# Attention by half-pairs: scores issued one half earlier on TensorE, copies of the turned probabilities one half later on ScalarE

## What is computed

```python
def one_block(args):                       # x tokens: 128 queries, local keys and context
    s_loc = jnp.where(mi, jnp.einsum('bqkgd,bskd->bkgqs', qi, ki), NEG_INF)
    s_ctx = jnp.einsum('bqkgd,bckd->bkgqc', qi, kc)
    p = jax.nn.softmax(jnp.concatenate([s_loc, s_ctx, sink_col], axis=-1), axis=-1)
    return (jnp.einsum('bkgqs,bskd->bqkgd', p[..., :n_loc], vi)
            + jnp.einsum('bkgqc,bckd->bqkgd', p[..., n_loc:n_loc + n_ctx], vc))
# context tokens: the same over the 256 context keys alone
...
mx = jnp.split((silu_c @ ada_w[i] + ada_b[i])[:, None, :], N_MOD, axis=-1)   # modulation
```

## Time and profile before

| What | us |
|---|---|
| median of 3 runs | 1977.81 (1974.31 to 1981.27) |
| the profiled execution | 1977.15 |
| its span on the profile | 1975.4 |
| PE busy | 1661.9 (84%) |
| DVE busy | 1138.1 (58%) |
| ACT busy | 855.2 (43%) |
| mean granted TensorE clock | 0.915 of full |
| the attention, first scores to first matmul of w_o | 126 to 331 |

### The profile page before, as it was taken

One profiled execution on the slowest core, in us unless ns is written; L12 is line 12 of the kernel. 1 busy time (PEld: TensorE's weight loads), 2 busy tenths in 40 slices (PEclk: granted clock), 3 DMA queues, 4 the chain that ended last, 5 costly groups with the idle time before them and its releaser, 6 DMA issues.

```text
span 1975.4 us, 23995 instructions
## 1 busy us (share of the span) xinstructions
PE 1661.9 (84%) x8586; PEld 1327.3 (67%) x8586; DVE 1138.1 (58%) x1780; ACT 855.2 (43%) x1286; POOL 16.8 (1%) x34
## 2 busy tenths in 40 slices
PE   3977777679999996888567999678787798998988
PEld 1853334568888885777456999566565686877768
DVE  2334444354444445678876666565546467777866
ACT  3223333442222333477554554424323265655653
POOL 1000000000000000000001000000000000000000
PEclk8988898879999998899787999778888699999999
DMA  8275552213323332132242666322211078878784
GB/s 304 70 295 175 193 212 85 65 33 96 106 87 104 96 96 64 43 97 85 74 128 88 189 187 184 111 71 83 78 55 41 29 239 274 283 259 272 264 287 160
DMA packets 201823, 279.57 MB, mean 142 GB/s; under 512 B 12314, under 2 KB 111116, under 8 KB 195596
## 3 DMA queue, kind: packets, MB, share of 16 engines
q1 hardware_dynamic: 200064, 269.90, 42.5%
q0 software_dynamic: 1152, 8.39, 1.1%
q10 hardware_dynamic: 524, 0.19, 0.0%
HBM read 277.40 MB, written 1.05 MB: 141 GB/s over the span
## 4 chain that ended last, share of the span: by engine, by line
PE 60%; DVE 21%; DMA 10%; ACT 6%; issue 3%; ACTq 0%; SPq 0%; DVEq 0%; POOL 0%; POOLq 0%
PE bank L390 47%; DMA stage<-in_w_dram 8%; DVE weights_lo L363 4%; PE bank L518 3%; ACT weights_hi L351 2%; PE bank L962 2%; DVE softmax_cols L1912 2%; DVE work L1932 1%; PE bank L946 1%; PE bank L1262 1%; PE bank L563 1%; DMA work<-in_c_ctx_dram 1%; DVE work L596 1%; DVE x_and_ctx L599 1%; PE bank L1312 1%
## 5 line engine op out<-in xcount | busy, mean ns | idle before, releaser
L363 DVE TENSOR_TENSOR weights_lo<-stage,weights_hi 128x1024 fp32r<-128x1024 f32 x428 | 515.8, 1222 | 158.7 <-ACT weights_hi L351 149.9
L351 ACT ACTIVATE weights_hi<-stage 128x1024 fp32r<-128x1024 f32 x428 | 442.4, 1056 | 231.6 <-DMA stage<-in_w_dram 120.6
L390 PE MATMUL bank<-act_hi,weights_hi 128*128 128x256 f32 (+1 forms) x976 | 317.4, 325 | 20.2 <-DVE x_and_ctx L2011 12.8
L390 PE MATMUL bank<-act_lo,weights_hi 128*128 128x256 f32 (+1 forms) x976 | 316.0, 324 | 0.0
L390 PE MATMUL bank<-act_hi,weights_lo 128*128 128x256 f32 (+1 forms) x976 | 315.6, 323 | 0.0
L390 PE MATMUL bank<-weights_hi,ff_hi 128*128 128x512 f32 x560 | 220.3, 393 | 11.5 <-DVE weights_lo L363 9.4
L390 PE MATMUL bank<-weights_hi,act_hi 128*128 128x512 f32 (+1 forms) x488 | 202.9, 416 | 31.7 <-DVE weights_lo L363 15.8
L390 PE MATMUL bank<-weights_hi,ff_lo 128*128 128x512 f32 x560 | 218.2, 390 | 0.0
L390 PE MATMUL bank<-weights_lo,ff_hi 128*128 128x512 f32 x560 | 218.1, 390 | 0.0
L390 PEld LDWEIGHTS bank<-act_hi,weights_hi 128*128 128x128 f32 x976 | 189.8, 194 | 36.0 <-issue 22.1
L390 PEld LDWEIGHTS bank<-act_lo,weights_hi 128*128 128x128 f32 x976 | 189.9, 195 | 13.6
(11 more groups left out here) (338 smaller groups left out, 1957.2 us busy)
## 6 DMA issues: line engine op xcount, KB each, us to landing
stage<-in_w_dram SPq DMA_DIRECT2D x192, 512.0 KB, 4.8
stage<-in_mlp_w_dram SPq DMA_DIRECT2D x128, 512.0 KB, 4.1
ada_rows_in<-in_ada_w_dram SPq DMA_DIRECT2D x40, 1024.0 KB, 5.1
stage<-in_w_in_dram SPq DMA_DIRECT2D x32, 512.0 KB, 4.0
stage<-in_lru_w_in_dram SPq DMA_DIRECT2D x20, 512.0 KB, 3.9
ada_rows_in<-in_ada_w_dram POOLq DMA_DIRECT2D x8, 1024.0 KB, 13.5
stage<-in_attn_w_qkv_dram SPq DMA_DIRECT2D x12, 512.0 KB, 5.0
stage<-in_lru_w_out_dram SPq DMA_DIRECT2D x10, 512.0 KB, 4.7
```

What stands on the lines that cost most here:

```text
L351: act.eng.activation(whi[u % NRING][:], stage[u % NSTAGE][:], ACT.Copy).then_inc(sem("hi_ready"), 1)
L363: dve.eng.tensor_tensor(wlo[u % NRING][:], stage[u % NSTAGE][:], whi[u % NRING][:].bitcast(F32), ALU.subtract).then_inc(sem("lo_ready"), 1)
L390: m = pe.eng.matmul(ps, l, r, start=start and j == 0, stop=stop and j == 2, skip_group_check=True)
```

## The change

On PE, `scores(0)` stands ahead of the loop and turn h issues `scores(h + 1)`. `values` of a pair moves from the odd turn to the even turn behind it, and the loop has one more turn. On ACT the copies of the turned half stand one turn later (half h-2 in turn h), and their wait for `values` moves with them. On DVE the split of the output moves to the even turn. The operations, their shapes, the buffers and the banks stay as they are.

```diff
--- before.py
+++ after.py
@@ -980,13 +980,14 @@
                                          skip_group_check=True)
                 m.then_inc(*pe.fill(("O", b)))
 
-            for h in range(34):
-                if h < 32:
-                    scores(h)
+            scores(0)
+            for h in range(35):
+                if h < 31:
+                    scores(h + 1)
                 if h - 1 in ADA_TURN:
                     ada_cols_pe(pe, ADA_TURN[h - 1], 7)
-                if h >= 3 and h % 2:
-                    values((h - 3) // 2)
+                if h >= 4 and h % 2 == 0:
+                    values((h - 4) // 2)
                 if 1 <= h < 33:
                     turn_probs(h - 1)
                 if h < 32:
@@ -1513,7 +1514,7 @@
                 turned_x(n)
                 if n < 2:
                     keep_ctx(n + 1)
-            for h in range(33):
+            for h in range(34):
                 if h < 32:
                     nk = P * len(key_tiles(HALVES[h][3]))
                     at = 2 * (h % 2)
@@ -1528,15 +1529,15 @@
                                      accum_out=sm[:, 1, at + i:at + i + 1]).then_inc(*act.free(("S", h, i)))
                     s.wait_ge(sem("sink_arg"), h + 1)
                     s.activation(sm[:, 2, at:at + 2], sm[:, 2, at:at + 2], ACT.Exp).then_inc(*act.mark("exps"))
-                if h:
-                    a = HALVES[h - 1][2]
-                    for n in range(len(key_tiles(HALVES[h - 1][3])) // 2):
-                        s.wait_ge(*act.filled(("PT", h - 1, n)))
-                        if h >= 3:
-                            s.wait_ge(*act.filled(("O", (h - 3) // 2)))
-                        ps = plan.bank(("PT", h - 1, n))
+                if h >= 2:
+                    a = HALVES[h - 2][2]
+                    for n in range(len(key_tiles(HALVES[h - 2][3])) // 2):
+                        s.wait_ge(*act.filled(("PT", h - 2, n)))
+                        if h >= 4:
+                            s.wait_ge(*act.filled(("O", (h - 4) // 2)))
+                        ps = plan.bank(("PT", h - 2, n))
                         s.activation(pT[:, 2 * n:2 * n + 2, a, :], ps[:].rearrange("p (k t) -> p k t", k=2),
-                                     ACT.Copy).then_inc(*act.free(("PT", h - 1, n)))
+                                     ACT.Copy).then_inc(*act.free(("PT", h - 2, n)))
                 if h in ADA_TURN:
                     ada_act(act, ADA_TURN[h])
                 if h == 28:
@@ -1931,8 +1932,8 @@
                     for i in range(2):
                         v.tensor_scalar(prob[g % 3][:, i, 0:nk], prob[g % 3][:, i, 0:nk], sm[:, 3, at + i:at + i + 1],
                                         None, ALU.mult).then_inc(*dve.mark("p_norm"))
-                if h >= 3 and h % 2:
-                    b = (h - 3) // 2
+                if h >= 4 and h % 2 == 0:
+                    b = (h - 4) // 2
                     j, c, _, qt = HALVES[2 * b]
                     v.wait_ge(*dve.filled(("O", b)))
                     ov = plan.bank(("O", b))[:, 0:256].rearrange("p (i t) -> p i t", i=2)
```

## The result

The changed kernel takes 1922.57 us (median of four runs, 1920.53 to 1923.48) against 1978.88 us of the kernel before on the same chip: the ratio is 0.9717, 95% interval 0.9697 to 0.9737. The profiled execution took 1921.84 us (span 1920.1), 55.3 us less than that of before.

The account below looks back on a forecast made before the run. Bound: the attention's ring of scores, maximum, scaling and turning, then TensorE's mixed clock. w_o at 285 instead of 331 us gains 46, less 4 for low clock: 42; 1977 - 42 = 1935 us, range 1923 to 1957.

Parts of the forecast that it names:

- everything behind 331 us moves along: Stages behind the attention, from w_o on, only start earlier; no gain or loss of their own was counted.
- the rest of the low level adds 4: Attention, 159 us from 126.3 to 285: remaining low-clock time adds 4 us, so the gain is 42.
- The ring and its cut: Attention: scores, maximum, scaling, turning wait in a loop, 6.33 us a long lap, 4.44 short; scores ahead remove it.
- The pair of turns: Attention: two long turns take 10.0 us instead of 12.66, two short ones 7.1 instead of 8.88.
- The three added waits: Attention: turning waits for copies, copies for values, odd maximum for DVE's output read; 0.7 us idle PE each turn.
- The parts of the sum: Attention at full clock: turn 4 at 142.8, turn 16 at 207, turn 30 at 270.4, w_o at 285 us.
- The clock: TensorE in the attention: granted clock near 0.97 instead of 0.88, PE's longest regular idle 0.7 us instead of 2.95.
- (1): Attention clock stays as mixed as now, 0.87: gain 22, 1955 us; chance 0.26 together with (2).
- (3): Attention slower: same ring with PE at its low level, 1984 us at clock 0.75; chance 0.04.
- (2): Attention hand-offs cost double or ACT is late: pairs 11.5 and 8.0 us, 1950 us; chance 0.26 together with (1).
- (4): Attention: bank 4 ties turn_probs(h-1) to exp(h), so laps stay: 1977 us; chance 0.04.
- (5): Attention better than written: full clock and hand-offs hidden, gain 46 + 9, 1922 us; chance 0.09.

Follow-up runs that it names:

- the filled kernel: Kernel before, in its own order, with needless matmuls into bank 4 while PE waits for the scaled probabilities: 1953.57 us, ratio 0.9887.
- the windows of 146 to 186 us shown above: From the kernel before with scores one half ahead, modulation steps ahead of turn_probs, and ACT's copy of the sums ahead of the turned half's: 1905.78 us, ratio 0.9643.

## Why the prediction was right, and where it was wrong

Two steps failed: *everything behind 331 us moves along* (8.0 us of the miss stand there), and *the rest of the low level adds 4* (these 4 us are most of the other 5.3). The mechanism of the change was right. Part by part:

*The ring and its cut*: right, and shown by three kernels. Scores ahead alone give the gain, the copies alone lose 27 us, and in the changed kernel the waits of L1912 and L962 moved as said.

*The pair of turns*: right. 9.77 us measured for 10.0 forecast, 6.85 for 7.1. The three added waits stand where the text put them, with 0.85 us of idle PE in the even turn and 0.34 in the odd one for my 0.7 in each. The pair is shorter in the odd turn, whose maximum starts with the even turning (159.09) and not 0.25 us behind it: DVE reads the output in 0.8 us (168.05 to 168.85) while PE waits 0.85.

*The parts of the sum*: turn 4 begins at 142.99 for 142.8; turn 16 at 206.19 for 207; turn 30 at 268.8 for 270.4; from there to w_o 15.0 us for 14.8. So w_o stands at 283.8 where the sum at the full clock said 285.

*The clock*: 0.96 for 0.97, right, but the 4 us that I added for it failed. The sum had low spells in it already (the first scores at the low level, 2 us behind the splits), and its pairs were rounded up: six long ones by 0.23 us and seven short ones by 0.25, 3.1 us in all. So even without the 4 us it stood 1.2 us above what was measured with all low spells in it. The measured low level lies at the start (0.50 from 126 to 131 us) and in the last third (0.83 from 260 to 270); from 136 to 240 us the clock was 1.00. The 4 us are most of the 5.3 by which the attention beat the forecast (47.3 gained, 42 forecast). That idle time causes the low level of before was argued from one row in the prediction; the filled kernel shows it. The measured 0.96 puts rivals (1) and (3) out.

*Everything behind moves along*: this is where most of the miss lies. The two profiled executions differ by 55.3 us where 42 were forecast: 8.0 of the 13.3 stand behind w_o, where I had nothing, and 5.3 in the attention. With only one of the two the time would have lain inside the range, at about 1931 or 1928 us. I took the stages behind w_o as fixed, 1644.3 us in the one profile I had. They vary by 9 us over the thirteen profiles, by 7.1 between the two of the kernel before, and the profile on record had a long one. So a part of the miss is luck: the changed kernel once more took 1925.09 us, inside the range, 51.2 less than before beside it. What is left without the luck of one execution is mostly the attention: in the means of two profiles each it fell from 207.2 to 158.4 us, 48.8 less and not 42, and the stretch behind from 1640.8 to 1636.5. Of these 4.3 us 1.4 are w_o's own start at the full clock, which the prediction had left out; for the rest two profiles each are too few. My range had nothing for the stretch behind, and its low end, 1923, came from the bounds of the attention alone.

*The rivals*: (2) was wrong, the hand-offs cost less than written. (4) was wrong. (5) named 1922 us, close to what came, but not by what came: it wanted the hand-offs hidden, and PE still waits 21.6 us for the copies. That the number fits is luck.

*What I didn't see*: that one of the two parts of the change, the later copies, only costs in this order of the steps. The prediction counted the 0.7 us of each turn as the price of the new waits but never asked what the scores ahead would give without the later copies. The same rows would have said 9.15 us a long pair; 9.02 came.

The prediction cites the Trainium skill (TensorE: Matmul & The Clock Gate, Part 4), by which a transpose doesn't count as activity for the full clock. That did not hold the clock down here: the turnings are as many as before and the clock rose to 0.96, and in the windows of 146 to 186 us shown above PE had the full clock with about a quarter of its time spent in them (9.8 of 40 us). No run here has a stretch of turnings alone.

## What to carry to other kernels

When an engine waits for a result of its own that comes back through two others, issue its next independent piece ahead of the dependent one and change nothing else at first: here that one edit on PE gave 1915 us, and the copies moved with it cost 6 to 10 us of it. Then fill the wait that is left with work that depends on neither, as the modulation steps did: about 20 us more in the changed kernel, about 7 in the one with the scores alone, after which both stand at 1901 to 1908 us. And before you forecast against one profile, ask how much the stages that the change doesn't touch vary.

## What the runs showed of the hardware

Adding matmuls made a kernel faster. With up to 20 needless matmuls a turn in PE's idle time (320 in all; 1417 matmuls and transposes in the attention for 1096) the granted clock there rose to 0.97 from 0.87 and 0.85 in two profiles of before, and the execution took 1953.57 us for 1974.33. In the kernel before, a turning behind 2.95 us of idle PE ran at the low level (1.97 us for 1.09), and its lap took 9.13 us at a clock of 0.63, where the next took 6.32 at 1.00.

The same instructions took 1635.2 to 1644.3 us in the stages behind the attention, over thirteen profiled executions of nine kernels that do not differ there. A part of it is the clock: w_o took 43.8 us at the full level from its first matmul on and 45.2 to 46.2 where it began at the low one, and behind the convolution the low level lasted about 6 us in one execution and about 3 in another. The rest is open.
